# A third opening chunk in the first projection of a two-block transformer kernel, and two small steps moved

## The reference

```python
mod = jax.nn.silu(c) @ w_ada[l] + b_ada[l]
sh1, sc1, ga1, sh2, sc2, ga2 = jnp.split(mod, N_MOD, axis=-1)

h = modulate(rms_norm(x, g_norm1[l]), sh1, sc1)
qa, ka, va, oa, gates, qb, kb, vb = jnp.split(h @ w_in[l], IN_SPLITS, axis=-1)
...
h_a = mlstm_bidirectional(q_a, k_a, v_a, g_a)
h_a = h_a * lax.rsqrt(jnp.mean(h_a * h_a, axis=-1, keepdims=True) + EPS)
...
h_b = from_heads(neighborhood_attention(to_heads(qb, NH_B), to_heads(kb, NH_B),
                                        to_heads(vb, NH_B), rpb[l])).astype(x.dtype)
mixed = jnp.concatenate([h_a, h_b], axis=-1) @ w_out[l]
```

## Time and profile before

| what | value |
|---|---|
| median of 3 runs | 2580.28 us (2579.51 to 2580.51) |
| profiled execution, its own time | 2586.97 us |
| span of its instructions | 2585.2 us |
| PE busy | 98% |
| DVE, ACT, POOL busy | 65%, 50%, 8% |
| mean granted TensorE clock | 0.998 |

### The profile page before, as it was taken

The page is one execution under the profiler, slowest core; times in us unless marked ns, Lnnn a source line. Parts: engine busy times, 40 slices in busy tenths (PEclk is TensorE's granted clock), DMA queues, the critical chain, the costliest instruction groups (busy, mean ns, idle before and its releaser), DMA issues.

```text
span 2585.2 us, 31168 instructions
## 1 busy us (share of the span) xinstructions
PE 2546.0 (98%) x11494; PEld 2069.8 (80%) x11494; DVE 1686.8 (65%) x1897; ACT 1295.0 (50%) x1613; POOL 213.1 (8%) x263
## 2 busy tenths in 40 slices
PE   7999999999999999999999999999999999999998
PEld 3887878878888888888888777888888888888887
DVE  4969879978777766655565678556655555555454
ACT  2454456445555555444544567454555555554443
POOL 0021133100000000000100135001000000000000
PEclk9999999999999999999999999999999999999999
DMA  9979978978888787666677644656666666666664
GB/s 371 410 255 343 307 253 269 341 220 270 275 261 268 218 219 211 188 205 205 192 228 219 179 139 139 187 192 206 193 215 207 205 201 207 199 213 201 192 194 154
DMA packets 374417, 591.55 MB, mean 229 GB/s; under 512 B 120980, under 2 KB 121356, under 8 KB 373804
## 3 DMA queue, kind: packets, MB, share of 16 engines
q1 hardware_dynamic: 348368, 518.59, 64.0%
q0 software_dynamic: 18928, 69.39, 7.9%
q10 hardware_dynamic: 7020, 2.26, 0.6%
HBM read 563.94 MB, written 2.10 MB: 219 GB/s over the span
## 4 chain that ended last, share of the span: by engine, by line
PE 87%; DVE 5%; DMA 3%; issue 2%; ACT 1%; SPq 1%; POOL 0%; DVEq 0%; ACTq 0%
PE gp L1626 27%; PE gp L1628 27%; PE gp L1627 27%; DVE w_lo L2175 2%; DVE ada_sum L2302 1%; DMA ada_ring<-in_w_ada_dram 1%; DMA proj<-in_w_ada_dram 1%; DMA raw<-in_w_in_dram 1%; DMA raw<-in_w_up_dram 1%; ACT w_hi L969 1%; PE tp L2077 0%; PE tp L1935 0%; PE tp L1786 0%; PE tp L1925 0%; PE tp L1711 0%
## 5 line engine op out<-in xcount | busy, mean ns | idle before, releaser
L2175 DVE TENSOR_TENSOR w_lo<-raw,w_hi 128x1024 fp32r<-128x1024 f32 x872 | 1072.9, 1235 | 754.8 <-ACT w_hi L969 752.1
L969 ACT CAST w_hi<-raw 128x1024 fp32r<-128x1024 f32 x872 | 911.3, 1050 | 988.9 <-PE gp L1628 801.8
L1626 PE MATMUL gp<-w_hi,h_hi 128*128 128x512 f32 x2636 | 1037.4, 394 | 6.7 <-DVE w_lo L2175 6.6
L1628 PE MATMUL gp<-w_hi,h_lo 128*128 128x512 f32 x2636 | 1026.4, 389 | 0.0
L1627 PE MATMUL gp<-w_lo,h_hi 128*128 128x512 f32 x2636 | 1026.3, 389 | 0.0
L1626 PEld LDWEIGHTS gp<-w_hi,h_hi 128*128 128x128 f32 x2636 | 495.1, 188 | 119.5 <-DVE w_lo L2175 10.3
L1628 PEld LDWEIGHTS gp<-w_hi,h_lo 128*128 128x128 f32 x2636 | 495.0, 188 | 104.3
L1627 PEld LDWEIGHTS gp<-w_lo,h_hi 128*128 128x128 f32 x2636 | 495.3, 188 | 100.6 <-issue 0.2
L1626 PE MATMUL gp<-w_hi,a_hi 128*128 128x512 f32 x704 | 274.3, 390 | 0.0
L1627 PE MATMUL gp<-w_lo,a_hi 128*128 128x512 f32 x704 | 273.9, 389 | 0.0
L1628 PE MATMUL gp<-w_hi,a_lo 128*128 128x512 f32 x704 | 273.9, 389 | 0.0
(11 more groups left out here) (339 smaller groups left out, 1439.9 us busy)
## 6 DMA issues: line engine op xcount, KB each, us to landing
raw<-in_w_in_dram SPq DMA_DIRECT2D x248, 512.0 KB, 4.5
raw<-in_w_up_dram SPq DMA_DIRECT2D x176, 512.0 KB, 4.6
raw<-in_w_ffn_in_dram SPq DMA_DIRECT2D x176, 512.0 KB, 4.4
ada_ring<-in_w_ada_dram POOLq DMA_DIRECT2D x128, 512.0 KB, 5.9
raw<-in_w_down_dram SPq DMA_DIRECT2D x88, 512.0 KB, 4.5
raw<-in_w_ffn_down_dram SPq DMA_DIRECT2D x88, 512.0 KB, 4.5
proj<-in_w_ada_dram SPq DMA_DIRECT2D x64, 512.0 KB, 9.3
raw<-in_w_out_dram SPq DMA_DIRECT2D x64, 512.0 KB, 5.2
```

The lines of the kernel that those rows point to most:

```text
L969: nc.scalar.copy(w_hi[:, s], raw[:, s]).then_inc(hi_ready, 1)
L1626: mm(o, hi[:, kt0 + kt, ps], w_hi[:, s, k, :], start=n == 0, stop=False)
L1628: return mm(o, lo[:, kt0 + kt, ps], w_hi[:, s, k, :], start=False, stop=n == g.kts - 1)
L2175: V.tensor_tensor(w_lo[:, s], raw[:, s], w_hi[:, s].bitcast(F32), ALU.subtract).then_inc(lo_ready, 1)
```

## The change

The opening takes three chunks (`g_first`), so that six blocks instead of four can be multiplied before the second quarter is there. The third chunk's accumulators are the banks 0 and 1 of `tp` (`open_bank`), since `gp` has two chunks' worth. Hence the transposes into these banks (kp 4, 5, 6) move behind b14, to where the third chunk is drained, and `keep_busy` multiplies in bank 3. SP loads b4 behind step 11 and b5 behind step 12 of the second quarter, and ACT drains the half chunks at the blocks `DRAIN_AT`. With `QUARTER_B` = 6 the additions of the second half begin two blocks later, with two more blocks of double additions. The heads' root moves on ACT from the second block of `g_in_o` to `k == HB + 1`, behind the last exponential, and the load of the exponential's table behind it is gone. Three additions of `ada_sum` leave `g_in_a1` (blocks 4, 5, 6 of it) and stand in `g_in_o` at blocks 1, 2, 3, and POOL's masks and loads are interleaved anew.

```diff
-    g_first = gemm(w_in, 2, kts=HK1, kind=OpenGemm)
-    g_in_a0 = gemm(w_in, 3 * WA // CW - 2, col0=2 * CW, kts=HK1)
+    g_first = gemm(w_in, 3, kts=HK1, kind=OpenGemm)
+    g_in_a0 = gemm(w_in, 3 * WA // CW - 3, col0=3 * CW, kts=HK1)
...
+        def open_bank(g, e):
+
+            return gp[g.bank(e)] if e < 2 else tp[:, 0:2]
...
-            return 2 if b in (10, 16, 22) else 1
+            return 2 if b in (10, 13, 16, 19, 22) else 1
...
-        IN_A1_ADA = [q for q in range(24) if q not in (1, 2, 3)]
+        IN_A1_ADA = [q for q in range(24) if q not in (1, 2, 3, 4, 5, 6)]
...
-        IN_O_ADA = list(range(4, 16))
+        IN_O_ADA = list(range(1, 16))
...
                 if n == HK1 - 1:
                     for blk in FRONT[:RING]:
                         load(*blk)
+                if n in (HK1 + 3, HK1 + 4):
+                    load(*FRONT[RING + n - HK1 - 3])
...
-            for blk in FRONT[RING:2 * RING]:
+            for blk in FRONT[QUARTER_B:QUARTER_B + RING]:
                 load(*blk)
...
             for n in range(HB):
                 if n == 4:
-                    ada_gate(n0)
+                    for m in range(3):
+                        ada_gate(n0 + m)
                 if n >= 4:
-                    ada_gate(n0 + n - 3)
+                    ada_gate(n0 + n - 1)
                 window(n)
...
+            DRAIN_AT = (11, 13, 15, 19, 23, 27)
...
-                if k == ML0 + HA * ML_H + 1:
-                    act.wait_ge(ml_ms, 1)
-                    nc.scalar.activation(hcol[:, 2, :], hcol[:, 1, :], ACT.Sqrt).then_inc(ml_rms, 1)
-                    act.preload_act_table_set("natural_log_exp_and_others")
...
+                if k == HB + 1:
+                    act.wait_ge(ml_ms, 1)
+                    nc.scalar.activation(hcol[:, 2, :], hcol[:, 1, :], ACT.Sqrt).then_inc(ml_rms, 1)
...
-                            keep_busy(4, tp[:, 0, 0:P])
+                            keep_busy(4, tp[64:P, 3, 0:P])
...
-                if b == QUARTER_B + 1:
+            def in_a0_each(i, e, j, first):
+                if first and j == 2:
+                    for t in range(ST):
+                        pe.wait_ge(drained[t], g_first.chunks)
                     transpose_x(0, (4, 5, 6), 0)
...
-            for n in range(HK1 + 2, DT):
+            weigh(HK1 + 2, 1)
+            for n in range(HK1 + 3, DT):
                 weigh(n, 1)
+                if n in (HK1 + 4, HK1 + 5):
+                    split(*FRONT[n - HK1])
             mod_part(HK1 // 2, HK1, 2)
-            split(*FRONT[4])
+            split(*FRONT[QUARTER_B])
             low_half(2)
-            split(*FRONT[5])
+            split(*FRONT[QUARTER_B + 1])
             low_half(3)
-            for b in range(RING, HALF_B):
-                if b >= RING + 2:
+            for b in range(QUARTER_B, HALF_B):
+                if b >= QUARTER_B + 2:
                     split(*FRONT[b])
-                for _ in range(halves_adds(b) + (4 if b == RING + 3 else 0)):
+                for _ in range(halves_adds(b) + (4 if b == QUARTER_B + 1 else 0)):
                     weigh(*late.pop(0))
```

More of the change, by code:

```diff
@@ L81, in order @@
         h = self.nb // 2
-        return [(e, j) for half in range(2) for e in range(2) for j in range(half * h, (half + 1) * h)]
+        return [(e, j) for half in range(2) for e in range(self.chunks) for j in range(half * h, (half + 1) * h)]
     def block(self, i, e, j):
@@ L704, in _ @@
             for b in range(-1, len(FRONT)):
-                if 4 <= b < len(FRONT) - RING:
+                if QUARTER_B <= b < len(FRONT) - RING:
                     load(*FRONT[b + RING])
-                elif b >= 4:
+                elif b >= len(FRONT) - RING:
                     load(g_in_a1, 0, 0, b + RING - len(FRONT))
@@ L892, in _ @@
                 if n == 4:
-                    ada_gate(n0)
+                    for m in range(3):
+                        ada_gate(n0 + m)
                 if n >= 4:
-                    ada_gate(n0 + n - 3)
+                    ada_gate(n0 + n - 1)
                 window(n)
-            for n in range(n0 + HB - 3, 2 * (DT - K1)):
+            for n in range(n0 + HB - 1, 2 * (DT - K1)):
                 ada_gate(n)
@@ L1123, in _ @@
             high_affine((1,))
-            split(*FRONT[2])
-            split(*FRONT[3])
+            for b in range(2, QUARTER_B):
+                split(*FRONT[b])
             act.wait_ge(row_summed, 2)
             nc.scalar.copy(half_rows[0:64], tp[0:64, 3, :]).then_inc(row_ready, 1)
-            split(*FRONT[4])
+            split(*FRONT[QUARTER_B])
             high_affine((2,))
-            split(*FRONT[5])
+            split(*FRONT[QUARTER_B + 1])
             high_affine((3,))
@@ L1138, in drain_half @@
                 for t in range(ST):
-                    nc.scalar.copy(first_proj(c_, t), as_proj(c_, gp[g.bank(e)][:, t, :])
+                    nc.scalar.copy(first_proj(c_, t), as_proj(c_, open_bank(g, e)[:, t, :])
                                    ).then_inc(drained[t], 1)
-            for b in range(RING + 2, HALF_B):
+            DRAIN_AT = (11, 13, 15, 19, 23, 27)
+            assert len(DRAIN_AT) == A0_CHUNKS
+            for b in range(QUARTER_B + 2, HALF_B):
                 split(*FRONT[b])
-                c_ = b // RING - 1
-                if c_ < A0_CHUNKS and b % RING == 3:
-                    drain_half(c_)
+                if b in DRAIN_AT:
+                    drain_half(DRAIN_AT.index(b))
             split(*FRONT[HALF_B])
@@ L1305, in in_o_each @@
             def in_o_each(i, e, j, first):
-                if first and j == 1:
-                    mlstm(heads_end + 1)
                 na_at(i, e, j, first)
@@ L1643, in parts @@
                     for k, t in pairs:
-                        last = mm(gp[g.bank(e)][:, t, :], lo[:, kt0 + kt + k, t * P:(t + 1) * P], w_hi[:, s, k, :],
+                        last = mm(open_bank(g, e)[:, t, :], lo[:, kt0 + kt + k, t * P:(t + 1) * P], w_hi[:, s, k, :],
                                   start=False, stop=False)
@@ L1833, in keep_busy @@
                 for _ in range(n):
-                    mm(o, ones[:, :], ones[:, :], start=True, stop=True)
+                    mm(o, ones[:, 0:o.shape[0]], ones[:, :], start=True, stop=True)
             for n in range(HK1):
@@ L2322, in weigh, with mod_part @@
                 ins.then_inc(done, 1)
-            def mod_part(a, b, done):
+            def mod_part(a, b, done, bank=3):
                 n = b - a
                 dve.wait_ge(mod_sum, done)
-                V.tensor_copy(mod[:, 0, a:b], tp[:, 3, 0:n])
-                V.scalar_tensor_tensor(mod[:, 1, a:b], tp[:, 3, n:2 * n], 1.0,
+                V.tensor_copy(mod[:, 0, a:b], tp[:, bank, 0:n])
+                V.scalar_tensor_tensor(mod[:, 1, a:b], tp[:, bank, n:2 * n], 1.0,
                                        vcol[:, 0, VC["g1"] + a:VC["g1"] + b],
```

18 lines of the change are left out of this document (8 added, 10 removed).

## The result

The changed kernel takes 2590.95 us (median of six, 2589.92 to 2593.54), the kernel before beside it 2580.4 (2578.25 to 2582.89). The ratio is 1.0040 with a 95% interval of 1.0028 to 1.0052: 10.3 us slower (7.2 to 13.4). The forecast was 2580.3 with a range up to 2585.3 and a chance of 0.08 for slower, so it was wrong. What happened is in the main the third rival, the one at which POOL's loads come too late for DVE; the forecast had given it 2588.4.

What follows compares the result with a forecast made beforehand. PE, busy 98% of the span, was taken as the bound. Opening +3.3, `g_in_a1` -2.4 and `g_in_o` -0.9 summed to 0.0 on the profiled 2586.97, carried to the median of 2580.28: 2580.3 us, range 2574.8 to 2585.3.

Steps and rivals of the forecast that it cites:

- the third rival: Start of `g_in_o`: POOL's `ada_ring` loads meet bias loads, land after 11.0 us; total +8.1, 2588.4 us, slower; chance 0.08.
- Opening, +3.3: Opening through b15: two blocks more before the second quarter, but a wait and half clock at b8; 3.3 us slower.
- six weighed pieces: DVE in front of b8: pieces taking 6.1 us together, ending at 79.1, so PE begins b8 at 80.6.
- upper bound of +4.0: Opening: the cost with a full dip to half clock and some late data, +4.0 us.
- a term of 1.4: b8 and b9: cost of the expected half-clock stretch, 1.4 us of a full 1.7, since it may begin within the wait.
- lower bound of 1.9: Opening: the cost without any dip to half clock, +1.9 us.
- `g_in_a1`, -2.4: `g_in_a1`: three additions leave DVE, PE's waits of 0.68 and 0.59 vanish; -2.4 us, bounds -1.5 and -3.5.
- `g_in_o`, -0.9: Start of `g_in_o`: PE's wait for ACT goes, DVE's additions and a late load take part back; b100 at 380.8, -0.9 us.
- I take 4.3: Start of `g_in_o`: assumed landing time of the load POOL issues at 370.7; 4.3 us, so landed at 375.0.
- dip of 1.4: Start of `g_in_o`, slower rival with chance 0.08: half-clock cost of 1.4 us added for PE's long waits.
- waits of 1.3 and 1.1 us: Second step of `g_in_o`: PE waits 1.3, then 1.1 us, for the first head's maximum and probabilities from DVE.
- 3.7 of the forecast's working: Start of `g_in_o`: the root's move saves PE's 2.7 us wait for ACT and about 1 of half clock.

Runs made afterwards that it cites:

- fill: The changed kernel with 15 multiplications of ones (128x128) added behind b7, in the wait in front of b8: 2588.42 us, ratio 1.0024 to before.
- opening: The kernel before with the third opening chunk alone; root and additions stand where they stood: 2584.59 us, ratio 1.0005 to before.
- rootada: The changed kernel without its opening change, so root and additions moved: 2588.48 us, ratio 1.0027 to before.
- ada: The kernel before with only the additions and POOL's loads moved as in the changed kernel: 2592.19 us, ratio 1.0035 to before.
- rootinter: The kernel before with root and three additions moved, POOL's three loads one each before the masks of windows 1, 2, 3: 2578.75 us, ratio 0.9985.
- openspread: The kernel before with the third opening chunk alone, DVE's four extra weighed pieces spread over b8, b9, b11, b12: 2582.1 us, ratio 1.0001.
- biaslater: rootada with ACT's bias loads of head 4 put behind head 1's exponentials: 2586.26 us, ratio 1.0023 to before.

## Why the prediction was wrong, point by point

**Opening, +3.3: right in its mechanism.** The geometry was met to 0.2 us (65.00, 80.59), and so was the cause of the wait, the six weighed pieces: 73.20 to 79.31. Counted from b0 the profile says +4.2 at b20, just over the upper bound of +4.0, because the half clock lasted 6.8 us instead of 3.4: b8 took 5.29 instead of 2.84, 2.4 for a term of 1.4. Where nothing was slowed behind the wait (`fill`, `opening`) it is 1.6 to 1.8, near the lower bound of 1.9 (whose sum makes 1.83). The place of the half clock differs between executions, and over three pairs the medians say 3.2.

**`g_in_a1`, -2.4: right.** From b40 to b60 the profile won 2.75 us, and 2.8 in `rootada`, `ada` and `rootinter`. The kernels whose additions stayed won 0.5 there too, so 2.2 is the additions'.

**`g_in_o`, -0.9: wrong, and the cause of the miss.** From b96 to b100 PE lost 6.6 us. The step that failed is the sentence "POOL now issues only behind the masks, which end at 370.7; ... I take 4.3: landed at 375.0". The wait itself was foreseen, and the forecast named its own failure: DVE waiting over 4 us there. It waited 9.76. Both numbers that set the length were off:

- The masks started as before (359.65, before 359.12), but ended at 375.0, 4.3 us later. Seven of the sixteen took 1.2 us or more where three had, and three of the seven (365.52, 366.96, 368.43) lie beside the three moved additions. I had taken the masks' end from the kernel before, although DVE beside them had three more additions to make; the last section has what the rows say of this.
- The landing took 7.7 us instead of 4.3. I took a low value since the DMA share was down to 0.29 in 368.3 to 371.7. That stretch lies before the loads are issued: it held the end of a block load and then nothing, and no packet of the bias loads, which moved from about 374 on in the kernel before. Its trace had the nearer row, the one load of `ada_ring` issued beside them, at 376.3: it took 8.1 us. The rival had the right mechanism, the bias loads. Its landing of 11.0 was counted from 370.7 and stands for what was in fact 4.3 of masks and 7.7 of landing, 12.0 together, so that its 2588.4 came near is in part luck. It also put the landing from which the whole is slower by over 5.2 us at 9.5; with the dip that it counts itself this is 8.1.

Together the load was there at 382.7 instead of 375.0, 7.7 later. b100 came 9.1 after its forecast; the other 1.4 lie behind the second maximum, mostly by the half clock there, the rival's "dip of 1.4": the four heads' parts before b100 took 4.35 us (385.52 to 389.87). In these 9.1 us is also that b96 itself began 1.5 us later than before, which the forecast counts in the stages ahead; the stage alone missed by 7.5, from -0.9 to +6.6.

The waits of 1.3 and 1.1 us that the forecast had in the second step came as nothing and 0.30 (373.00). DVE's three additions began at 365.31, 0.95 earlier than the forecast had them, and PE came to that step later. This changed nothing, since the load came last.

**The root's part** of that stage was right: ACT had copied the first head's q and k at 365.3 and PE's 2.68 us were gone. Measured alone it is worth 4.4 us, near the 3.7 of the forecast's working. But `opening` and `openspread` have no such wait either, so in the changed kernel, beside the third chunk, the forecast may have counted as a gain of the root what the opening had taken away already.

**Carrying to the median.** With +6.6 in `g_in_o` the forecast's sum would have been +7.5, or 2587.8; with all three stages as the profiles have them it is +8.0. Measured were 10.3 with an interval of 7.2 to 13.4, so the 2 to 3 us between are not told from chance.

In the medians the parts add up: +3.2 for the opening, -4.4 for the root, +11.4 for the additions beside it make 10.2, where 10.3 was measured. This proves less than it seems, since the last two are together `rootada`'s 7.0, and one of the three pairs behind 3.2 is the changed kernel against `rootada`. With the other two pairs, +1.3 and +4.9, the sum is 8.3 and 11.9. The +1.3 is the one pair with the root in its old place, where the profiles have PE's wait gone with the opening; the difference to the others is within the uncertainty.

The Trainium skill, "DMA: Bandwidth & Descriptors", Why small descriptors are slow (HBM only), says that descriptors of about 256 bytes carry overhead; the page's example puts it at 27% for 256 bytes. The rows of the changed kernel agree in direction, but the size differs: 31 GB/s at 35% of the engines' time is some 88 GB/s of full time, where the stretch of block loads at 79.5 to 86.3 has 365 GB/s at a share of 1.02. The measurement decides. The same page, Queues, rings and completion order, says that a DMA engine takes turns between the queues that have work. Here the block load issued at 371.9 had no packet up to 376, while those of the bias loads passed; from 376 to 379.3 both queues moved (223 and 173 packets). Why the turns did not come sooner is open.

## What to carry to other kernels

A load that an engine issues behind its own work has two arrival times to estimate, its issue and its landing, and both depend on what the change puts beside them: ask what slows the work in front, and look for the loads that are issued just ahead of it, at their packets' size and rate, and not at the DMA share of the stretch before. Moving work off a stage where an engine is a little late pays only if the place where it goes is not on a chain, DVE's start of the attention here. A single profiled execution can be several us off its kernel's median, and a wait that one profile shows can be gone in the next kernel for another reason. A part of the change tried alone (the root: a few lines moved, -4.4 us) tells more than the whole.

## What was not expected of the hardware

- A POOL mask of 64x288 took 0.45 us or 1.24 to 1.77 in the first sixteen of the changed kernel. With three additions more on DVE seven instead of three of the sixteen were long. The traces of all 13 kernels from 340 to 460 us have 132 masks of over 1 us, and 131 of them began while an addition or a low part of DVE ran; 127 of these took what that instruction had still to run and 0.32 us more (365.52: the addition had 1.06 left, the mask took 1.38). So a mask that begins beside such an instruction ends behind it. No run tried this by itself.
- Half clock came in stretches of 3.4, 6.8 and 10.2 us. The longest, 379.9 to 390.1, began some 3 us into PE's wait and went on for 4.6 us after its work had begun again (385.52); in `biaslater` a wait of 5.2 us had one of 10.2 us as well. The Trainium skill, "TensorE: Matmul & The Clock Gate", Part 1, calls the half clock the state of an idle engine; that the clock stayed full at b8 in `fill`, whose only difference are the ones in the wait, agrees. It is one execution, and where the half clock lies differs between executions: `opening` had it ahead of a wait of 1.86 us and none behind, without any ones.
- While the bias loads passed, loads of 512 KB took 7.7 to 9.5 us, in `rootada` up to 10.4; without them, in `biaslater`, 4.2 to 7.5.
